# A first projection with chunked modulation, rows scaled by a diagonal product, and head norms folded by VectorE and spread by DMA

## What is computed

```python
mod = silu(c) @ w_ada + b_ada                 # 1024 x 6144
sh1, sc1, g1, sh2, sc2, g2 = split(mod, 6)
h = rms_norm(x, norm1_g) * (1 + sc1) + sh1
proj = h @ w_in                               # 1024 tokens x 2208 columns
q, k, v, c_q, c_kv, k_rope, conv_in = split(proj)
q, k = rms_norm(q per head of 64), rms_norm(k per head of 64)
c_q, c_kv, k_rope = rms_norm over 384, 256 and 32 columns
```

## Time and profile before

| | us |
|---|---|
| median of 3 runs | 3150.15 |
| lowest and highest of them | 3148.28, 3152.46 |
| the profiled execution | 3145.51 |
| its span in the trace | 3143.9 |
| TensorE busy in it | 2966.0 |

### The profile page before, as it was taken

How to read it: one execution, slowest core, us unless ns; L and a number is a source line. 1 busy time by engine, 2 the same in 40 slices (tenths; PEclk the granted TensorE clock), 3 DMA queues, 4 the chain that set the end, 5 groups by cost and what they waited for, 6 DMA issues and landing times.

```text
span 3143.9 us, 40427 instructions
## 1 busy us (share of the span) xinstructions
PE 2966.0 (94%) x16581; PEld 2317.6 (74%) x16581; DVE 1729.3 (55%) x1883; ACT 1010.0 (32%) x1309; POOL 420.9 (13%) x461
## 2 busy tenths in 40 slices
PE   2998999999999999999998999999979999999989
PEld 2886666667788888888777887878767886666667
DVE  5534635663445545543495747557454226676784
ACT  2122535552211111111233424225232114444452
POOL 0002010000111111100101102021111001333340
PEclk7999999999999999999999999999978999999999
DMA  6334110010133333321114233242311322212121
GB/s 228 116 112 113 24 31 17 20 28 28 54 101 113 118 116 100 113 87 48 41 54 123 82 88 107 67 127 81 99 62 34 107 81 67 68 34 63 39 73 62
DMA packets 244027, 245.89 MB, mean 78 GB/s; under 512 B 13317, under 2 KB 207714, under 8 KB 243874
## 3 DMA queue, kind: packets, MB, share of 16 engines
q1 hardware_dynamic: 220160, 167.07, 17.6%
q0 software_dynamic: 17680, 58.89, 6.3%
q10 hardware_dynamic: 6034, 17.74, 1.4%
HBM read 214.89 MB, written 26.40 MB: 77 GB/s over the span
## 4 chain that ended last, share of the span: by engine, by line
PE 79%; DVE 11%; issue 4%; ACT 3%; DMA 2%; ACTq 0%; SPq 0%; POOL 0%; DVEq 0%; POOLq 0%
PE PU L942 16%; PE PU L944 16%; PE PU L943 16%; PE PM L1601 2%; PE PU L1579 2%; PE PU L1271 2%; DVE small L2709 2%; PE PM L1589 2%; PE PM L1621 2%; PE PM L1623 2%; DMA seg<-decay_sums 2%; PE PM L1622 2%; PE PU L956 1%; PE PU L1202 1%; PE PU L957 1%
## 5 line engine op out<-in xcount | busy, mean ns | idle before, releaser
L942 PE MATMUL PU<-hH,w_hi_t 128*128 128x512 f32 (+1 forms) x1872 | 740.0, 395 | 2.4 <-DVE w_lo_t L2327 2.4
L944 PE MATMUL PU<-hH,w_lo_t 128*128 128x512 f32 (+1 forms) x1872 | 731.2, 391 | 0.0
L943 PE MATMUL PU<-hL,w_hi_t 128*128 128x512 f32 (+1 forms) x1872 | 730.4, 390 | 0.0
L2327 DVE TENSOR_TENSOR w_lo_t<-w_raw,w_hi_t 128x1024 fp32r<-128x1024 f32 x181 | 228.1, 1261 | 433.3 <-ACT w_hi_t L1733 421.2
L942 PEld LDWEIGHTS PU<-hH,w_hi_t 128*128 128x128 f32 (+1 forms) x1872 | 351.6, 188 | 77.5 <-DVE w_lo_t L2327 3.8
L944 PEld LDWEIGHTS PU<-hH,w_lo_t 128*128 128x128 f32 (+1 forms) x1872 | 351.1, 188 | 76.2
L943 PEld LDWEIGHTS PU<-hL,w_hi_t 128*128 128x128 f32 (+1 forms) x1872 | 351.6, 188 | 72.0
L1733 ACT ACTIVATE w_hi_t<-w_raw 128x1024 fp32r<-128x1024 f32 x167 | 174.6, 1045 | 457.4 <-PE PU L944 356.4
L2777 DVE SCALAR_TENSOR_TENSOR xT<-PU,mod,xT 128x1024 f32<-128x1024 f32 x120 | 154.0, 1284 | 201.0 <-PE PU L944 201.0
L3057 DVE TENSOR_TENSOR_SCAN s_keep<-s_keep,zero 128x128 f32<-128x128 f32 (+7 forms) x128 | 180.6, 1411 | 2.0 <-POOL s_keep L897 2.0
L897 POOL TENSOR_SCALAR_AFFINE_SELECT s_keep<-s_keep 128x128 f32<-128x128 f32 x128 | 114.4, 910 | 501.5 <-ACT s_keep L2215 500.9
(11 more groups left out here) (420 smaller groups left out, 5026.4 us busy)
## 6 DMA issues: line engine op xcount, KB each, us to landing
ada_w<-in_ada_w_dram POOLq DMA_DIRECT2D x64, 384.0 KB, 4.1
w_raw<-in_w_gu_dram SPq DMA_DIRECT2D x44, 512.0 KB, 3.7
w_raw<-in_m_in_w_dram SPq DMA_DIRECT2D x40, 512.0 KB, 3.8
ada_w<-in_w_ada_dram POOLq DMA_DIRECT2D x32, 512.0 KB, 4.5
seg<-decay_sums SPq DMA_DIRECT2D x32, 512.0 KB, 4.3
w_raw<-in_w_down_dram SPq DMA_DIRECT2D x22, 512.0 KB, 3.3
w_raw<-in_w_in_dram SPq DMA_DIRECT2D x17, 512.0 KB, 3.8
ada_w<-in_w_ada_dram SPq DMA_DIRECT2D x16, 512.0 KB, 19.4
```

The source lines that it names most:

```text
L942: mm(PU[0:width, up, half, :], whi, aH[:, k, cols], start=k == 0, stop=False)
L943: mm(PU[0:width, up, half, :], whi, aL[:, k, cols], start=False, stop=False)
L944: last = mm(PU[0:width, up, half, :], wlo, aH[:, k, cols], start=False, stop=k == kt - 1)
L2327: V.tensor_tensor(w_lo_t[:, p, 0:w], w_raw[:, p, 0:w], w_hi_t[:, p, 0:w].bitcast(F32), ALU.subtract)\
```

## The change

It has two parts.

The beginning. POOL zeroes the vectors' stage first. ScalarE's queue loads the two rows of c, then x; the two vectors c alone are turned first, so that silu(c) is taken at once. SP's queue loads the 2048 columns of `w_ada` as four chunks, each with 256 columns of the shift and 256 of the scale (4 DMAs of 512 KB, runs of 1 KB): chunks 0 and 1, two panels, chunks 2 and 3. The other vectors come by 8 DMAs on ScalarE's queue and 16 on POOL's. Spread and row scaling go: VectorE makes 8 diagonal matrices of the inverse roots (`inv_diag`), TensorE multiplies x tile by tile with them into `PM` (`normalised`, 8 float32 matmuls for a feature tile, in place of a transposition of its own), and ScalarE applies scale and shift and then makes the high part; VectorE is left with the low part. `xT` is still made, for later. The sum over the partitions of a chunk is 4 matmuls with a column of ones (`ada_chunk_columns`) in place of transpose and reduction. VectorE's work on chunks 2 and 3 is placed between the low parts of tiles 0 to 4, and `feat_pair` takes the `normalised` jobs ahead of its steps. POOL's slabs wait for all four chunks; its write of the bias rows moves behind the eighth slab.

The norms. `column_sums`, `head_spread` and the spreads of cq, ckv and krope go. VectorE folds the squares of a unit by a 32x32 transpose and a reduction to 128x32 (`squares_folded`), TensorE adds the quarters with 1 to 3 matmuls of 32 columns in the middle of the next unit (`norm_sums`; none for krope), ScalarE takes the root of 128x32, VectorE the inverse and a transpose; SP's queue stores the rows to DRAM and loads them back spread over the partitions into `n_bc` (`norm_rows`), between its panels, and VectorE scales the unit by `n_bc`.

The diff, cut to its core:

```diff
+            def ada_chunk(j):
+                for half in range(2):
+                    for s in range(2):
+                        c0 = s * D + 256 * j
+                        sp.dma_start(ada_w0[:, half, j, :, s, :], w_ada[:, 4 * half:4 * half + 4, c0:c0 + 256])\
+                            .then_inc(ada0_landed[j], 16)
+            for j in range(2):
+                ada_chunk(j)
...
+            def norm_rows(e):
+                kind, _ = NORMS[e]
+                n = NORM_ROWS[e]
+                r0 = 64 if kind == "krope" else 0
+                sp.wait_ge(g_turn, e + 1)
+                for r in range(n):
+                    sp.dma_start(scr_n[r, :].rearrange("(j c) -> j c", c=32), g_turned[r0 + HD * r:r0 + HD * r + 32, 0, :]).then_inc(g_store, 16)
+                sp.wait_ge(g_store, 16 * sum(NORM_ROWS[:e + 1]))
+                if e:
+                    sp.wait_ge(j_done, e)
+                rows = 32 if kind == "krope" else P // n
+                for r in range(n):
+                    sp.dma_start(n_bc[r0 + rows * r:r0 + rows * (r + 1), :], scr_n[r:r + 1, :].broadcast_to([rows, T])).then_inc(g_land, 16)
             w_in = a["w_in"].rearrange("o (k p) c -> p (o k) c", p=P)
-            for kind, t, c0 in WIN_UNITS:
+            for n, (kind, t, c0) in enumerate(WIN_UNITS):
                 panel(w_in[:, :, c0:c0 + (ROPE if kind == "krope" else P)], KD, ROPE if kind == "krope" else P)
+                if n == 1:
+                    for j in (2, 3):
+                        ada_chunk(j)
+                if n >= 4 and WIN_UNITS[n - 4][0] in ("q", "k"):
+                    norm_rows(NORMS.index(WIN_UNITS[n - 4][0:2]))
             w_out = a["w_out"].rearrange("o (k p) c -> p (o k) c", p=P)
             for t in range(2):
                 panel(w_out[:, :, t * P:(t + 1) * P], KD, P)
-            stored = 0
+                norm_rows(4 + t)
+            norm_rows(6)
...
+                if b == 2:
+                    g.dma_start(scr_bias, rp[0:nrow, :].unsqueeze(1).broadcast_to([nrow, GRID, P])).then_inc(rp_landed, 16)
...
+            def norm_sums(e):
+                kind, t = NORMS[e]
+                slots = [FOLDS.index((kind, k)) for k in range(t + 1)] if kind in ("cq", "ckv") else [FOLDS.index((kind, t))]
+                pe.wait_ge(sq_fold, slots[-1] + 1)
+                roots_read()
+                sel = fold64 if kind in ("q", "k") else fold
+                for n, f in enumerate(slots):
+                    last = mm(PM[:, 0, 0:32], sel[:, :], h_red[:, f % 4, :], start=n == 0, stop=n == len(slots) - 1)
                 last.then_inc(stat_done, 1)
-            def head_spread():
-                pe.wait_ge(c_inv, cr.next())
-                for t in range(TT):
-                    for hd in range(2):
-                        last = mm(PM[hd * HD:(hd + 1) * HD, t // 4, (t % 4) * P:(t % 4 + 1) * P],
-                                  rt[:, 0, 2 * t + hd:2 * t + hd + 1].broadcast_to([P, HD]), ident[:, :], start=True, stop=True)
-                last.then_inc(c_bc, 1)
+                roots_.next()
...
+            def ada_chunk_columns(j):
+                pe.wait_ge(ada_acc_s, job.next())
+                if j >= 2:
+                    pe.wait_ge(ada_mod, j)
+                for n in range(4):
+                    last = mm(PM[:, 3, 4 * j + n:4 * j + n + 1], ada_acc0(j)[:, n * P:(n + 1) * P], ones[:, 0:1], start=True, stop=True)
+                last.then_inc(ada_col, 1)
+            def normalised(k):
+                if k == 0:
+                    pe.wait_ge(c_inv, cr.next())
+                else:
+                    pe.wait_ge(h_hi, k)
+                for t in range(TT):
+                    last = mm(PM[:, t // 4, t % 4 * P:(t % 4 + 1) * P], x_stage[:, t, k * P:(k + 1) * P], inv_diag[:, t, :],
+                              start=True, stop=True)
+                last.then_inc(xn_ps, 1)
...
+            pe.wait_ge(vec_dma, 16 * len(first_rows))
+            pe.wait_ge(vec_dma2, 16 * (len(more_rows) + len(vec_parts)))
             pe.wait_ge(cact_done, 1)
-            spread(rt[:, 0, :])
-            for _ in range(2):
-                ada_columns()
+            for n in range(NVEC):
+                last = nc.tensor.transpose(PM[:, 2, n * P:(n + 1) * P], v_stage[:, n, :], ident[:, :])
+            last.then_inc(vec_t, 1)
+            normalised(0)
+            for j in range(2):
+                ada_chunk_columns(j)
             pe.wait_ge(x_ev[0], TT // 2)
             pe.wait_ge(x_ev[1], TT // 2)
-            feat_pair(hr())
+            ahead = {k - 1: [lambda k=k: normalised(k)] for k in range(1, KD)}
+            ahead[2].append(lambda: ada_chunk_columns(2))
+            ahead[4].append(lambda: ada_chunk_columns(3))
+            feat_pair(hr(), ahead=ahead)
...
-                prior, pt_, _ = WIN_UNITS[n - 1]
-                if prior in ("q", "k"):
-                    head_spread()
-                    normed.next()
-                if (prior, pt_) in (("cq", 2), ("ckv", 1)):
-                    spread(rt[:, 0, :])
-                    normed.next()
-                if kind in ("q", "k"):
-                    later.append(lambda: column_sums(blk64[:, 0:P:HD]))
                 if kind == "v":
                     later.append(lambda t=t: values_transposed(t))
-                if kind == "cq":
-                    if t == 0:
+                if (kind, t) in NORMS and kind != "krope":
+                    if kind == "cq":
                         later.append(lambda: pe.wait_ge(nv_tok, 2))
-                    later.append(lambda t=t: column_sums(ones[:, 0:1], first=t == 0, final=t == 2))
-                if kind == "ckv":
-                    later.append(lambda t=t: column_sums(ones[:, 0:1], first=t == 0, final=t == 1))
+                    later.append(lambda e=NORMS.index((kind, t)): norm_sums(e))
                 if n in ADA_AT_UNIT:
                     ada_columns()
-            column_sums(blk96[64:96, 64:65], bank=0, rows=ROPE, r0=64)
...
+            act.wait_ge(pchain, 1)
+            for b, r0, rows, width, src in c_rows:
+                act.dma_start(v_stage[r0:r0 + rows, b, 0:width], src).then_inc(c_dma, 16)
+            x_v = a["x"].rearrange("o (t p) d -> p (o t) d", p=P)
+            for t in range(TT):
+                act.dma_start(x_stage[:, t, :], x_v[:, t, :]).then_inc(x_landed[t // 2], 16)
             act.wait_ge(vec_t, 1)
-            act.wait_ge(vec_done, 1)
-            af(cact[:, :], v("c", 0, 16), ACT.Silu).then_inc(cact_done, 1)
+            af(cact[:, :], PM[:, 2, 2 * P:2 * P + 16], ACT.Silu).then_inc(cact_done, 1)
+            for b, r0, rows, width, src in first_rows:
+                act.dma_start(v_stage[r0:r0 + rows, b, 0:width], src).then_inc(vec_dma, 16)
...
+            for k in range(KD):
+                act.wait_ge(xn_ps, k + 1)
+                act.wait_ge(ada_mod, k // 2 + 1)
+                if k >= 2:
+                    act.wait_ge(h_ready, k - 1)
+                link(af(n_h[:, k % 2, :], stat_ps, ACT.Identity, bias=m("sh1", k), scale=coef[:, 0, k:k + 1]))
+                af(hH[:, k, :], n_h[:, k % 2, :], ACT.Copy).then_inc(h_hi, 1)
...
+            def norm_root(e):
+                kind, _ = NORMS[e]
                 cr.next()
-                af(rt[:, b, 0:cols], PM[:, 0, 0:cols], ACT.Sqrt, bias=EPS, scale=scale).then_inc(c_root, 1)
+                if e:
+                    act.wait_ge(g_turn, e)
+                if kind == "krope":
+                    act.wait_ge(sq_fold, len(FOLDS))
+                    src = h_red[64:96, (len(FOLDS) - 1) % 4, :]
+                    ins = af(n_rt[64:96, :], src, ACT.Sqrt, bias=EPS, scale=1 / ROPE)
+                else:
+                    act.wait_ge(stat_done, e + 1)
+                    ins = af(n_rt[:, :], PM[:, 0, 0:32], ACT.Sqrt, bias=EPS, scale={"cq": 1 / QR, "ckv": 1 / KVR}.get(kind, 1.0))
+                ins.then_inc(c_root, 1)
+            def head_square(dst, src):
+                if stat.n:
+                    act.wait_ge(sq_fold, stat())
+                stat.next()
+                af(dst, src, ACT.Square).then_inc(sq_ready, 1)
...
+                ve.wait_ge(ada_col, max(2, job.next()))
+                for s in range(2):
+                    c = 8 * s + 2 * j
+                    ins = V.tensor_tensor(mod[:, c:c + 2], PM[:, 3, 4 * j + 2 * s:4 * j + 2 * s + 2], v("b_ada", c, 2), ALU.add)
+                link(ins)
+                V.scalar_tensor_tensor(coef[:, 0, 2 * j:2 * j + 2], m("sc1", 2 * j, 2), 1.0, v("norm1_g", 2 * j, 2),
+                                       ALU.add, ALU.mult).then_inc(ada_mod, 1)
...
+            ada_chunk(0, range(KD))
+            x_moved(1)
+            x_moved(3)
+            ada_chunk(1, range(4))
+            x_moved(5)
+            ada_chunk(1, range(4, KD))
+            ve.wait_ge(c_root, cr.next())
+            link(V.reciprocal(rt[:, 0, 0:TT], rt[:, 0, 0:TT]))
+            for t in range(TT):
```

(51 more changed lines are left out.)

236 lines of the change are left out of this document (116 added, 120 removed).

## The result

The changed kernel takes 3125.55 us (median of 4 runs, 3124.56 to 3127.54) against 3149.68 (4 runs, 3148.28 to 3152.46): a ratio of 0.9928 with a 95% interval of 0.9916 to 0.9941. It is 24.1 us faster where 31.8 were forecast. The profiled execution is the slowest of its four, 3127.54 us.

What follows compares the result with a forecast made beforehand. TensorE was taken to bound the kernel (busy 2966 of 3143.9 us), VectorE its beginning. Norms 25.8 plus beginning 6.0 make 31.8 us off the median of 3150.15: 3118.4 us, range 3108 to 3133.

Steps and rivals of the forecast that it cites:

- Norms: Projection and krope's spread: 26.4 us of norm work leave TensorE, 2.5 come new, 1.9 for krope's spread; net 25.8 us.
- The store and the load: Norm rows through DRAM on SP's queue: store lands in 1.4 us (at most 3.1), load in 3.8; a miss costs VectorE.
- The end of the projection: After krope's unit: the folds make VectorE reach the bias tables later, by nothing to 0.5 us.
- The beginning: Start to end of first pair: first product at 44 in place of 70, pair ended at 87.6 against 93.6; 6.0 us gained.
- if the queues share by bytes, chunk 0 is there at 12: DMA of the beginning: x and `w_ada` on two queues; chunk 0 lands at 12, the last of x at 25.
- rival (b): Beginning's DMA: x lands first, at 18, chunk 0 not before; all behind it 3.3 us later, 3121.7; 18 in 100.
- both gaps: TensorE's idle before 44 and near 54: half speed after the first adds 2.1 us, after both 4.8.
- The stand at chunk 2: First pair: VectorE stands at chunk 2's modulation until TensorE's column job, 54 to 55; TensorE idles some 5 us.
- Rival (a): The beginning gives nothing: chain for each tile, VectorE's stand at chunk 2 and slow clocks; 3124.4; 12 in 100.
- (c): Projection: VectorE's fold comes after the unit's middle; TensorE stands 1 to 2 us in 6 to 9 units; 3128; 8 in 100.
- (e): Projection: SP stands at the store's landing with panels behind it; slower than before, 3155 at 16 us each; 3 in 100.
- (f): Norms: the spread norms only move, TensorE had to stand just as long; within 0.2%, 3146; 3 in 100.

Runs made afterwards that it cites:

- fold_doubled: The changed kernel with each fold's transpose and reduction on VectorE done twice: 3130.02 us, ratio 0.9948.
- norms_alone: The kernel before with only the norms changed and the beginning as before: 3126.03 us, ratio 0.9932.
- kept_busy: The changed kernel with 28, 24 and 32 extra transposes, results unread, where TensorE would wait: 3119.31 us, ratio 0.9919.
- around_spread: The changed kernel with VectorE scaling rows instead of the diagonal product, chunks 0, 1 and x's halves alternating on one queue, column sums ahead of the spread: 3106.11 us.
- beginning_alone: The kernel before with only the beginning changed and the norms as before: 3149.79 us, ratio 1.0007.
- x_behind_chunk0: The changed kernel with x's eight DMAs on the queue of `w_ada`, between chunk 0 and chunk 1: 3124.35 us, ratio 0.9929.
- combined: The changed kernel with VectorE scaling rows instead of the diagonal product, evacuation ahead of chunk 0, x behind chunk 0, extra transposes ahead of spread and products: 3114.92 us.

## Where the prediction was right, and where it wasn't

**Norms: right, and by its own steps.** Forecast were 23.9 us in the projection and 1.9 for krope's spread; the projection gave 24.4, and from the last product of neighbourhood attention to the first of latent attention it is 1.5 us in place of 3.4, from start to start. Squares are 11.58 us apart (11.3 forecast, 14.84 before) where a column job lies between them, and 11.15 where none does. A sum of the quarters takes 0.30 us for a group of two and TensorE stands for no fold. VectorE's timeline shows the cover: the fold ends at 155.05, TensorE's sum of it starts at 157.16, 2.1 us later, and the next ones are 1.7 apart (166.63, 168.31). 1.9 was forecast, and `fold_doubled` confirms it from the other side: with 2.47 us more TensorE stands 0.33 and 0.75 us ahead of the same two sums, which is nearly 2.47 less 2.1 and 2.47 less 1.7.

```profile
152.55 1.25 DVE L2596 STREAM_TRANSPOSE ada_acc<-j_sq 128x1024 f32<-128x1024 f32 x1 [5.92 <-ACT j_sq L1919]
153.83 1.22 DVE L2597 TENSOR_REDUCE h_red<-ada_acc 128x32 f32<-128x1024 f32 x1
154.97 1.22 DVE L2417 TENSOR_TENSOR w_lo_t<-w_raw,w_hi_t 128x1024 fp32r<-128x1024 f32 x1
```

The store and the load were too rosy. The eleven stores landed in 1.3/3.5/6.3 us (least, median, most), where 1.4 was taken, the loads in 3.6/4.3/6.7 us, not 3.8, and VectorE waited 7.0 us for them in 4 scalings (under 2 forecast). It cost TensorE nothing, as the prediction said of such a miss.

**The end of the projection: right in size.** VectorE reaches the bias tables 8.96 us behind krope's unit, 8.52 before: 0.4 us, within "nothing to 0.5".

**Behind the projection: not all arrived in the profiled execution.** The two landmarks of krope's end are 22.0 us apart (298.60 and 276.60). The last neighbourhood product starts 79.05 us behind it (355.66), and 75.77 before. TensorE's stand for the bias tables is in one piece now; before, spread and sums lay in it and the longest piece was 6.06 us:

```profile
290.71 2.08 PE L1214 MATMUL PU<-na_k,na_q 64*128 64x512 f32 x4 [11.86 <-DVE small L2697]
```

The clock from 30 to 40 us behind the unit was 0.66 in the changed kernel's trace and 0.83 before. That the removed norm work is the cause isn't shown: four other traces with the changed norms have 0.83 there (`norms_alone`, `fold_doubled`, `kept_busy`, `around_spread`), and `beginning_alone`, with the old norms, has 0.66. But it goes with the time: from krope's end to the first decay sums it is 1371.7 to 1374.6 us in the five traces with 0.83 and 1377.1 to 1378.7 in the eight with 0.66 or 0.67.

The parts of the two profiled executions so add up: 24.4 won in the projection, less 2.4 in the beginning, 3.6 between krope's end and the decay sums and 0.4 in the last part is 18.0, the difference of the spans (3143.9 and 3125.9). The medians are 24.1 apart, because the profiled execution before was 4.2 us faster than the median of its kernel and the one after 2.0 slower. That 24.4 and 24.1 are so near is chance.

**The beginning: wrong, 0.2 to 2.4 us lost where 6.0 won were forecast.** The steps, in the prediction's order, as the changed kernel's trace has them:

| step | forecast | measured |
|---|---|---|
| chunk 0 landed | 12 | 19.1 |
| diagonals ready | 34.0 | 38.4 |
| first normalised chunk done | 35.9 | 42.3 |
| column sums of chunks 0 and 1 done | 36.5 | 45.5 |
| first product | 44.0 | 52.7 |
| VectorE let go at chunk 2 | 54 to 55 | 62.5 |
| third low part done | 58.1 | 66.9 |
| each tile after that | 4.6 | 4.5 |
| pair ended | 87.6 | 96.0 |

The step that failed first is "if the queues share by bytes, chunk 0 is there at 12". The DMA's totals (queue, kind: packets, MB, share of 16 engines) of the first 12 and of the first 19.1 us are these; q1 carries `w_ada`, q10 x:

```profile
q1 hardware_dynamic: 1767, 1.76, 45.2%
q10 hardware_dynamic: 492, 1.70, 36.7%
...
q10 hardware_dynamic: 1061, 3.77, 51.4%
q1 hardware_dynamic: 2339, 2.33, 37.1%
```

Between the two, x's queue moved 569 packets and `w_ada`'s 572: one for one. In bytes it was 2.07 MB against 0.57, since x comes in rows of 4 KB and `w_ada` in runs of 1 KB. That the totals of the first 12 us are nearly equal in bytes is the start: in the first 7 us `w_ada`'s queue moved 1360 packets and x's 88, and from then to 19.1 it was 979 against 973. This is rival (b), which had 18 in 100, though not to the letter: it had x whole at 18, and ScalarE's squares waited for x until 23.3. By the Trainium skill, "DMA: Bandwidth & Descriptors", section "Queues, rings and completion order", an engine takes a whole packet from each queue in turn; the trace agrees, with 569 against 572. With x on the same queue behind it, chunk 0 is there at 9.35. Rival (b) priced it at 3.3 us, and `x_behind_chunk0` gives 2.6 to 3.95 back by the second unit. The 3.3 don't follow from the rival's own times: with the evacuations ended at 26.4 the first half of chunk 1 starts 1.4 us later than the 25 of the forecast.

The second is a consequence that no step and no rival had: VectorE's order. In the forecast chunk 0 came ahead of x's second group of transposes. When it came late, VectorE waited for it with the evacuation queued behind, and TensorE stood 6.61 us. Moving that one copy brings the diagonals 1.8 us sooner (1.9 counted from chunk 0), and the second unit 2.0 to 3.3. That this and the gain of the landing add isn't shown; both act ahead of the diagonals.

The third is a size: the column sums were put at 0.6 us for two chunks. They took 3.41, and 1.84 to 1.89 where the clock was at its upper level, so 1.3 us were mis-sized and 1.5 are the clock. The first normalised chunk took 3.78 in place of 1.94, at a granted clock of 0.50. The prediction had both steps at the upper level and added half speed at the end, 2.1 us for the first gap. `kept_busy` prices the clock of the whole beginning at 3.4 to 5.1 us, where the prediction had put both gaps at 4.8 and taken 3.0 of it.

The stand at chunk 2 was foreseen (5 us; 4.53 for TensorE and 5.72 for VectorE), and so were the 4.5 us a tile. What the prediction didn't ask is whether the stand could be seen as a fault of the order: one step sooner gives 6.4 us, more than the stand itself, because the time at the lower clock behind it goes too.

**Rivals and range.** The time is inside the range of 3108 to 3133, 7.2 us above the 3118.4. That it is inside owes to the range, which took in a beginning worth nothing, and not to the steps: of the two parts one came as forecast and the other didn't come. Rival (a), "the beginning gives nothing", 3124.4, is what came, and by its own mechanism: chain for each tile, stand and slow clock, with (b) on top. It had 12 in 100. The fold wasn't late (c), SP's stores didn't hold the panels (e), and the norms' gain is real (f).

## What to carry to other kernels

Where two queues load at the same time, reckon their shares in packets: here rows of 4 KB took 2.07 MB beside the 0.57 MB of runs of 1 KB. What is needed first goes on the same queue, ahead. An engine's in-order list must follow the order of landing, and filler work in such a list must end before its next real work is due: in `combined` the inverse roots were there 2.4 us sooner and stood behind 28 transposes. And a removed stand is worth more than its length where TensorE comes out of it at the lower clock (6.4 us for one of 4.53 on TensorE and 5.72 on VectorE); for a product that replaces work on another engine, add up what it puts in series with the products of each tile.

## What the runs showed of the hardware

- Eight float32 matmuls of one column (two chunks' sums, 16 instructions in the trace) took 3.41 us in one execution and 1.84 at the upper level of the clock, some 0.12 us an instruction. They are hardly cheaper than eight of 128 columns, which took 1.95. Three executions of the same beginning had 3.41, 1.84 and 3.41.
- Transposes whose results nobody reads, in the stands of TensorE, kept the clock at 1.00 from 40 to 80 us, where it had been 0.65 and 0.83, and the second unit starts 4.3 us sooner with 84 transposes more (3.4 to 5.1 counted from chunk 0). Twenty-eight of the same, ahead of a spread that was due, held it back by 3.0 us (`combined`).
- A DMA store of the inverse norms landed in 1.3/3.5/6.3 us and a spreading load in 3.6/4.3/6.7 us (the mixer's, before, 1.3/1.4/3.1 and 3.5/3.8/4.2). In the projection, where ten of the eleven are, the DMA share was 0.56.
- From 30 to 40 us behind krope's unit the granted clock was 0.83 in five traces and 0.66 or 0.67 in eight, and the stretch of some 1375 us that it opens was 2.5 to 7.0 us longer in the eight. What decides between the two is open.
